# Second attention of a two-block kernel: the values' projection, the norm and the next logits taken into the pairs

## Reference, cut to what matters

```
proj = rms_norm(h, norm1_g) @ w_in_2
a_b, a_c, a_h, q, k, v, c_u, c_v = split(proj)
q = rms_norm(q per head, q_norm_g) ; k = rms_norm(k per head, k_norm_g)
for each block of 128 queries:
    z = (q @ k.T) / 8                     # keys up to the block's end
    log_beta = log_sigmoid(z)
    log_rem  = where(s < t, log_sigmoid(-z), 0)
    suffix   = reversed cumulative sum of log_rem, exclusive
    weights  = where(s < t, exp(log_beta + suffix), 0)
    o = weights @ v
```

## Time and profile before

| what | value |
|---|---|
| runs | 2827.7, 2827.54, 2825.6 us; median 2827.54 |
| profiled execution | 2826.8 us, its span 2824.7 us |
| mean granted clock of PE | 0.993 |
| PE busy | 2744.4 us, 97% of the span |
| DVE, ACT, POOL busy | 1892.2 (67%), 1006.8 (36%), 1187.7 us (42%) |
| chain that ended last | PE 82%, DVE 8%, issue 3%, POOL 3%, ACT 3%, DMA 1% |
| second attention | about 1588.7 to 1865.3 us of the span |

### The profile page before, as it was taken

One profiled execution on the slowest core, in us unless ns is written; L12 is line 12 of the kernel. 1 busy time (PEld: TensorE's weight loads), 2 busy tenths in 40 slices (PEclk: granted clock), 3 DMA queues, 4 the chain that ended last, 5 costly groups with the idle time before them and its releaser, 6 DMA issues.

```text
span 2824.7 us, 37570 instructions
## 1 busy us (share of the span) xinstructions
PE 2744.4 (97%) x14914; PEld 2208.4 (78%) x14914; DVE 1892.2 (67%) x2244; ACT 1006.8 (36%) x1482; POOL 1187.7 (42%) x705
## 2 busy tenths in 40 slices
PE   8999999989899999999999999999999999999999
PEld 6888777767778888888878666678778888888887
DVE  7677577677866777766768777655865545555555
ACT  5455433332422222222253455432332332232251
POOL 3111100002466766667764311132555555555553
PEclk9999999999999999999999999999999999999999
DMA  3111011121111111111112100012111111111112
GB/s 123 33 42 35 31 46 45 38 85 40 41 49 53 57 60 49 53 49 56 60 57 97 46 23 24 23 43 99 45 50 55 49 56 49 52 53 49 60 60 74
DMA packets 62760, 148.99 MB, mean 53 GB/s; under 512 B 7881, under 2 KB 8705, under 8 KB 62593
## 3 DMA queue, kind: packets, MB, share of 16 engines
q1 hardware_dynamic: 58272, 132.58, 14.9%
q10 hardware_dynamic: 4320, 14.09, 1.3%
HBM read 135.77 MB, written 8.52 MB: 51 GB/s over the span
## 4 chain that ended last, share of the span: by engine, by line
PE 82%; DVE 8%; issue 3%; POOL 3%; ACT 3%; DMA 1%; SPq 0%; ACTq 0%; DVEq 0%; POOLq 0%
PE ps L987 8%; PE ps L989 8%; PE ps L988 8%; PE ps L1109 8%; PE ps L1111 8%; PE ps L1110 8%; PE ps L1150 6%; PE ps L1152 6%; PE ps L1151 6%; PE ps L1274 2%; POOL ss L879 1%; PE ps L1490 1%; PE ps L1500 1%; PE ps L1514 1%; PE ps L1368 1%
## 5 line engine op out<-in xcount | busy, mean ns | idle before, releaser
L987 PE MATMUL ps<-a_hi,w_hi 128*128 128x512 f32 x1184 | 492.2, 416 | 10.6 <-POOL w_lo L856 10.0
L851 POOL TENSOR_TENSOR w_hi<-w_raw,der 128x1024 fp32r<-128x1024 f32 (+1 forms) x57 | 105.9, 1858 | 885.3 <-PE ps L989 766.3
L989 PE MATMUL ps<-a_hi,w_lo 128*128 128x512 f32 x1184 | 465.9, 393 | 0.0
L988 PE MATMUL ps<-a_lo,w_hi 128*128 128x512 f32 x1184 | 465.1, 393 | 0.0
L898 POOL TENSOR_TENSOR w_lo<-w_raw,w_hi 128x512 fp32r<-128x512 f32 x214 | 324.5, 1519 | 268.4 <-ACT w_hi L2457 268.4
L2132 DVE TENSOR_TENSOR x<-ps,x 128x512 f32<-128x512 f32 x432 | 295.4, 689 | 149.4 <-PE ps L1152 146.2
L2457 ACT ACTIVATE w_hi<-w_raw 128x512 fp32r<-128x512 f32 (+1 forms) x251 | 170.3, 680 | 540.1 <-PE ps L1152 238.0
L987 PEld LDWEIGHTS ps<-a_hi,w_hi 128*128 128x128 f32 x1184 | 224.6, 190 | 60.3 <-issue 17.5
L989 PEld LDWEIGHTS ps<-a_hi,w_lo 128*128 128x128 f32 x1184 | 223.9, 189 | 49.2
L988 PEld LDWEIGHTS ps<-a_lo,w_hi 128*128 128x128 f32 x1184 | 225.0, 190 | 37.3 <-issue 0.2
L898 POOL TENSOR_TENSOR w_lo<-asum,w_hi 128x512 fp32r<-128x512 f32 x114 | 166.6, 1461 | 185.0 <-ACT w_hi L2457 185.0
(11 more groups left out here) (395 smaller groups left out, 6113.5 us busy)
## 6 DMA issues: line engine op xcount, KB each, us to landing
w_raw<-in_w_mix SPq DMA_DIRECT2D x54, 512.0 KB, 3.7
w_raw<-in_w_f SPq DMA_DIRECT2D x96, 256.0 KB, 2.6
w_raw<-in_w_gu SPq DMA_DIRECT2D x88, 256.0 KB, 2.6
w_raw<-in_w_ple SPq DMA_DIRECT2D x16, 512.0 KB, 3.6
chunk<-in_w_f SPq DMA_DIRECT2D x32, 256.0 KB, 3.0
chunk<-in_w_dn SPq DMA_DIRECT2D x22, 256.0 KB, 3.0
w_raw<-in_w_dn SPq DMA_DIRECT2D x22, 256.0 KB, 3.0
x<-in_x SPq DMA_DIRECT2D x8, 512.0 KB, 7.5
```

Source lines behind the costliest of these rows:

```text
L987: mm(ps[:, bank, :], wh, hi[:, k, cols], start=(k == 0), stop=False)
L988: mm(ps[:, bank, :], wh, lo[:, k, cols], start=False, stop=False)
L989: last = mm(ps[:, bank, :], wl, hi[:, k, cols], start=False, stop=(k == nk - 1))
```

## The change

- `sb_fill` gives three units instead of two to the slots of pairs 0 to 2, so the next pair's values' unit is filling too (48 steps); `sb_slots` gives 3 steps to each of slots 0 to 7, 2 to slots 8 to 11, 1 to slots 12 to 15, 2 to slots 16 and 17 and 1 to slots 18 to 25.
- The block between pairs is gone from PE's list. What it did for pair 0 stands once ahead of the loop.
- ACT squares q in round 4 and k in round 6 and takes the root at the end of round 8. PE sums the squares in slot 14 (round 7) into bank 1. DVE takes the mean in round 7, the reciprocal in round 9 and the two multiplications at the end of round 11.
- For pairs 1 to 3 the factors are no longer spread by matmuls: SP writes them to DRAM after the reciprocal and reads them back with four transfers of 256 KB each (1 MB in all, 64 partitions by 4 pieces of 1 KB) into a new tile `spread_qk` of 8 KB a partition, which DVE's multiplications read in place of PSUM.
- The next pair's first two logits are made in round 12 as soon as q and k are ready, ahead of the last slot; in round 0 the first slot's filling comes ahead of the transposes of the values for pairs 1 to 3.
- SP's loop over the weights of this stage is written out, and waits for the factors ahead of the load of a values' unit.

```diff
 def sb_fill(p):
-    return (U_SB + 3 * (p + 1), 2) if p + 1 < HEADS else (U_CV, 3)
+    return (U_SB + 3 * (p + 1), 3)
 ...
-    return [[steps.pop(0) for _ in range(2 if i < 2 or 15 <= i < 19 else 1)] for i in range(n)]
+    counts = [3] * 8 + [2] * 4 + [1] * 4 + [2] * 2 + [1] * 8
+    return [[steps.pop(0) for _ in range(m)] for m in counts]
+S_SUM = 14
 ...  SP
-            weights("w_mix2", U_SB, U_OUT2 - U_SB)
+            def spread_qk_factors(p):
+                sp_.wait_ge(st_inv, N_QK + p + 1)
+                sp_.dma_start(qk_factors[p - 1].rearrange("r g c -> (r g) c"), hsm[0:P:8, :]).then_inc(qk_fac_out, 16)
+                sp_.wait_ge(qk_fac_out, 16 * p)
+                sp_.wait_ge(qk2_ready, 2 * p)
+                for t in range(2):
+                    for hh in range(2):
+                        src = qk_factors[p - 1, :, 2 * t + hh, :].rearrange("(o r) c -> o r c", o=1)
+                        sp_.dma_start(spread_qk[64 * hh:64 * hh + 64, t, :].rearrange("p (r c) -> p r c", r=4),
+                                      src.to_broadcast([64, 4, T // 4])).then_inc(qk_fac_in, 16)
+            for u in range(U_SB, U_OUT2):
+                p, t = divmod(u - U_SB, 3)
+                if t == 2 and 2 <= p <= HEADS:
+                    spread_qk_factors(p - 1)
+                sp_.wait_ge(w_split, u - 1)
+                sp_.dma_start(w_raw[:, u % 2, :], io["w_mix2"][u - U_SB]).then_inc(w_in[u % 2], 16)
 ...  PE, in round n of pair p
+                    if n == 0:
+                        if p:
+                            norm_fill(p, slots[0])
+                        pe.wait_ge(acc_free, half_no(u + 2, 1))
+                        pe.wait_ge(swt_ready, 2 * NSEG * p)
+                        pe.wait_ge(so_out, 2 * p)
+                        transposes(sv, 6, sv_tr)
+                        if p == 0:
+                            norm_fill(p, slots[0])
+                        norm_fill(p, slots[1])
+                        continue
                     for hh in range(2):
-                        if 1 <= n <= NSEG:
+                        if n <= NSEG:
                             turn(p, n - 1, hh)
-                        if n <= NSEG:
+                        if n == NSEG and hh and more:
+                            pe.wait_ge(qk2_ready, 2 * p + 4)
+                            logits(p + 1, 0)
+                            logits(p + 1, 1)
+                        if n <= NSEG and more:
+                            norm_fill(p, slots[2 * n + hh])
+                            if 2 * n + hh == S_SUM:
+                                pe.wait_ge(sq_qk, 2 * p + 4)
+                                pe.wait_ge(acc_free, half_no(u + 4, 1))
+                                head_sums(1)
+                        elif n <= NSEG:
                             fill(slots[2 * n + hh])
 ...  DVE, after the weights of round n
+                    if p + 1 < HEADS:
+                        if 2 * n == S_SUM:
+                            head_mean(N_QK + p + 1, 1)
+                        elif 2 * n == S_SUM + 4:
+                            head_factor(N_QK + p + 1)
                     evict(slots[2 * n] + slots[2 * n + 1], u_next, next_)
+                    if p + 1 < HEADS and 2 * n == S_SUM + 8:
+                        dve.wait_ge(qk_fac_in, 64 * (p + 1))
+                        for t, gain in enumerate((dcol("qn"), col("kn"))):
+                            stt(sk[(p + 1) % 2][:, t, :], sk[(p + 1) % 2][:, t, :], gain, spread_qk[:, t, :],
+                                ALU.mult, ALU.mult).then_inc(qk2_ready, 1)
 ...  ACT, end of round n
-                    if n == 10 and p + 1 < HEADS:
-                        square(p + 1, 0)
-                if p + 1 < HEADS:
-                    square(p + 1, 1)
+                    if p + 1 < HEADS:
+                        if n in (4, 6):
+                            square(p + 1, n // 2 - 2)
+                        elif n == 8:
+                            head_sqrt(N_QK + p + 1)
```

More of the change, by code:

```diff
@@ L95 @@
 SPREAD = tuple(range(N_DA, N_HG + HEADS - 1))
+SPREAD_QK = tuple(range(N_QK + 1, N_QK + HEADS))
 def bc_no(n):
-    return n + 1 - len([m for m in SPREAD if m <= n])
+    return n + 1 - len([m for m in SPREAD + SPREAD_QK if m <= n])
 F_MIX = 0
@@ L416, in bass_two_blocks @@
         hsm = at("hsm", T // 4, S0 + 57 * KB)
+        spread_qk = at("spread_qk", (2, T), -15 * KB)
         past = at("past", T, TMP)
@@ L486, in bass_two_blocks @@
         x_back = nc.dram_tensor("x_back", (P, KT, T), F32, kind="Internal").ap()
+        qk_factors = nc.dram_tensor("qk_factors", (HEADS - 1, 4, 4, T // 4), F32, kind="Internal").ap()
         factors = nc.dram_tensor("factors", (len(SPREAD), KT, P), F32, kind="Internal").ap()
@@ L512, in bass_two_blocks @@
         fac_in = sem("fac_in")
+        qk_fac_out = sem("qk_fac_out")
+        qk_fac_in = sem("qk_fac_in")
         guarded = sem("guarded")
@@ L1039, in gemm_loop, with head_sums @@
                         gemm(u0 + 2 * i + s, s, hi, lo, nk, wait_k if s == 0 else None)
-            def head_sums():
+            def head_sums(bank=7):
                 for g, src in enumerate((c_buf, ss)):
                     for r in range(4):
-                        last = mm(ps[32 * r:32 * r + 32, 7, 0:256], heads[g], src[:, 256 * r:256 * r + 256],
+                        last = mm(ps[32 * r:32 * r + 32, bank, 0:256], heads[g], src[:, 256 * r:256 * r + 256],
                                   start=g == 0, stop=g == 1, skip_group_check=True)
@@ L1517, in values, with norm_fill @@
                 last.then_inc(so_mm, 2)
+            def norm_fill(p, slot):
+                for step in slot:
+                    if step == (U_SB + 3 * (p + 1) + 2, 1, 0):
+                        pe.wait_ge(st_var, N_QK + p + 2)
+                    fill([step])
+            gemm_half(U_SB + 2, 1, U_SB % 2, a_hi, a_lo, KT, end=3)
+            pe.wait_ge(sq_qk, 2)
+            head_sums()
+            gemm_half(U_SB + 2, 1, U_SB % 2, a_hi, a_lo, KT, first=3, end=6)
+            pe.wait_ge(xf_ready, 1)
+            head_bcast(N_QK)
+            gemm_half(U_SB + 2, 1, U_SB % 2, a_hi, a_lo, KT, first=6)
+            pe.wait_ge(qk2_ready, 2)
+            logits(0, 0)
+            logits(0, 1)
             for p in range(HEADS):
                 u = U_SB + 3 * p
[L1521 to L1536, removed]
+                more = p + 1 < HEADS
                 slots = sb_slots(p)
[L1538 to L1541, removed]
                 for n in range(NSEG + 2):
@@ L1662, in prep, with head_mean, head_factor, head_inverse @@
                 tt(ss[:, :], ss[:, :], sq[:, k % 2, 0:T], ALU.add).then_inc(ss_ready, 1)
-            def head_inverse(n):
+            def head_mean(n, bank=7):
                 dve.wait_ge(st_sum, n + 1)
-                ts(hsm[:, :], ps[:, 7, 0:256], 1.0 / 64, EPS, ALU.mult, ALU.add).then_inc(st_var, 1)
+                ts(hsm[:, :], ps[:, bank, 0:256], 1.0 / 64, EPS, ALU.mult, ALU.add).then_inc(st_var, 1)
+            def head_factor(n):
                 dve.wait_ge(st_root, n + 1)
                 nc.vector.reciprocal(hsm[:, :], hsm[:, :]).then_inc(st_inv, 1)
+            def head_inverse(n):
+                head_mean(n)
+                head_factor(n)
             def row_inverse(n, scale):
@@ L2343, in _ @@
             dve.wait_ge(tri_in, 32)
-            for p in range(HEADS):
[L2345 to L2353, removed]
+            leave_half(U_SB + 2, 0, sv[:, :], 4)
+            head_inverse(N_QK)
+            dve.wait_ge(st_bc, bc_no(N_QK))
+            for t, gain in enumerate((dcol("qn"), col("kn"))):
+                stt(sk[0][:, t, :], sk[0][:, t, :], gain, banks(4 - 2 * t), ALU.mult, ALU.mult).then_inc(qk2_ready, 1)
+            leave_half(U_SB + 2, 1, sv[:, :])
+            dve.wait_ge(x_out, 16 * KT)
+            for p in range(HEADS):
                 slots = sb_slots(p)
@@ L2356, in _ @@
                 if p + 1 < HEADS:
-                    next_ = [sk[(p + 1) % 2][:, 0, :], sk[(p + 1) % 2][:, 1, :]]
+                    next_ = [sk[(p + 1) % 2][:, 0, :], sk[(p + 1) % 2][:, 1, :], sv[:, :]]
                 else:
                     next_ = [cc[:, j, :] for j in range(3)]
-                dve.wait_ge(x_out, 16 * KT)
                 for n in range(NSEG + 1):
@@ L2366, in _ @@
                         weights(p, n, 1)
-                    evict(slots[2 * n] + slots[2 * n + 1], u_next, next_)
+                    if p + 1 < HEADS:
[3 more added lines that the diff above has]
+                            head_factor(N_QK + p + 1)
+                    evict(slots[2 * n] + slots[2 * n + 1], u_next, next_)
+                    if p + 1 < HEADS and 2 * n == S_SUM + 8:
+                        dve.wait_ge(qk_fac_in, 64 * (p + 1))
+                        for t, gain in enumerate((dcol("qn"), col("kn"))):
+                            stt(sk[(p + 1) % 2][:, t, :], sk[(p + 1) % 2][:, t, :], gain, spread_qk[:, t, :],
```

(5 more changed lines are left out.)

## The result

The changed kernel takes 2836.63 us (median of 6 runs, 2834.72 to 2839.78) against 2825.85 us before in the same comparison: 1.0037 times as long, 95% interval 1.0027 to 1.0047. That is 10.8 us slower, where no measurable change (2823.8) was forecast, and above the range of 2816.5 to 2832.

A forecast was written before the change was run, and what follows sets the result against it. PE, busy 97% of the span, was taken as the bound: periods of 69.55 us against 70.70 give -3.45 over three, the last pair -0.3, so -3.75 and a median of 2823.8 us, range 2816.5 to 2832.

The forecast's parts named there:

- the transfer: Factors through DRAM to DVE's multiplications in round 11: 8.3 us from reciprocal to use, 7.95 available, so 0.35 us late.
- the upper bound of 11.9: Highest estimate of the factors' way through DRAM, if a 1 KB packet takes as long as an average 2.3 KB one.
- The first block's 5.38 us: Precedent in the profile before: from reciprocal to what waits for it, 512 KB in rows of 4 KB.
- the sum: A period of 65.0 + 0.35 + 3.85 + 0.35 = 69.55 us against 70.70; with the last pair -3.75 us in all.
- The price of a late transfer: At pair ends: slower by over 5.7 us only from about 3 us late; below that nothing measurable changes.
- the far end: Factors 3.95 us late: period 73.15 us, plus 1.6 us of slow clock each time, +11.9 us in all, 2839.
- Rival 2: The four factor transfers come late at DVE's round 11 multiplications, up to 2839 us; chance 0.10 from 3 us on.
- The tail: Rounds 8 to 13 of a pair: DVE has no rest and PE waits for it; 3.85 us a period.
- The last pair: Final pair of the stage: loses its 0.85 us table load, has thinner first slots; -0.3 us kept.
- Rival 1: DVE doesn't bound rounds 8 to 13: period 66.1 us, 2813.4 in all, half way 2818.5; chance 0.37 with half way.
- Rival 3: Each ACT table switch costs about 1.4 us more than its load: +4.6 us in all, 2832; chance 0.02.
- rival 4: Waits in mid-pair (values' unit half 1, squares in round 6) hold PE up; ends at no change; chance 0.03.

## Why the prediction was wrong

**The step that failed is the transfer**, "so I take 8.3". From the end of the reciprocal to DVE's use it measured 11.0, 9.8 and 11.3 us, so the upper bound of 11.9 was the nearer one. The pieces, for pair 1: 1.8 for the write, 1.95 until the last of four reads is issued (about 0.65 each), 6.0 from there to landing; in pair 0 3.5, 2.0 and 5.4. The first block's 5.38 us had one read and one short write in it, and I had put only a little more than the bytes on top of it. Bytes and issues together are shown by the run with half the reads, pieces of 1 KB (0.1 to 1.1 us) by that with 4 KB rows, and the load behind them (0.3 to 0.9 us), of which the sum says nothing, by the one with its order turned. So DVE was late by 2.2 to 3.7 us, not 0.35.

**The price of a late transfer was too low as well.** I counted the clock's 1.6 us a time at the far end, 3.95 us late, but the sentence that nothing measurable changes below about 3 us leaves it out: at 2.9 us late the terms of the sum give 3 x 1.4 - 0.3 = +3.9 us, and with the clock, which I had seen fall after 3.48 us of standing still, +8.7. It fell after 3.25, 2.10 and 1.91 us too (after the last, with half the reads, a pair's first to third logits took 9.53 us instead of 8.01). Without that, the direct lateness alone (PE's waits sum to 12.4 us against 2.8 without the transfer, 9.6 more) would have used up the gain of 4.9 and left 4.7; with 5.8 of clock it is 10.5, against 10.8 measured. Rival 2 is what happened. I had put 2839 at its far end and gave it a chance of 0.10 from 3 us on. It deserved far more: the estimate stood on one precedent of half the size, and its upper bound lay beyond that point.

**The tail was right for DVE.** Zero at the start of round 9 (1710.94 in the profile after): the scans of segment 9 were put at 2.85 and came at 2.98, the end of the reciprocal at 8.35 and 8.3, the last weights at 16.3 and 15.9. At the turn of segment 10 PE waited 0.56 us instead of 1.4: it came there 0.6 later than I had it, not least by a wait of 0.64 at the turn of segment 8, where ACT's copy stands behind the table loads and which the walk of PE leaves out. Without lateness the sum gives a period of 69.20 and -4.8 us; without the transfer 68.94 and -4.9 were measured. That the two agree so closely is partly luck: two errors nearly cancel. PE's waits are 2.1 us a pair (0.64, 0.57 and 0.93) instead of my 3.2 (1.4, 0.3 and 1.5), and what PE needs beside them is 66.8 instead of 66.0. The table loads had their share in it (5.8 us) and the reciprocal too (5.5), each taken away alone. That the block's removal would pay for itself only just, since DVE becomes the bound at the pair's end, is shown.

**The last pair** went as put: without the transfer, its 66.22 us from first logits to the end hold 0.69 and 1.02 moved in from the pair before, which leaves 64.5 against 64.80, -0.3. In the changed kernel the slow clock at its start makes it 68.01.

**Rival 1** (the tail isn't bound by DVE) was wrong for the change as made and right for what could be made of it: with the reciprocal moved into DVE's idle time, periods of 67.4 and 66.95 us against its 66.1. **Rival 3** (a drain at each table switch) and **rival 4** (waits in mid-pair) are excluded by the timelines: no gap after a load, no wait of PE in rounds 0 to 8 of pairs 1 and 2.

## What to carry to other kernels

A result that goes through DRAM has a due time: add the write up to its landing, each issue and the last read's landing separately, at the size and number they have, and put its producer where its engine idles anyway, several us before the need. When PE bounds the kernel and has to stand still even for some 2 us, count the slow stretch behind it too; here it cost 5.8 us on top of 9.6 of waiting. And where a list is moved into the shadow of another, walk the engine that gets the new work to the end of the stage: it may become the bound in the last rounds although on average it has a quarter of its time free (54.3 of 73.7 us busy here).

## What the runs showed of the hardware

- In this stage the granted clock fell after PE had stood still for 1.91, 2.10 and 2.52 us and in all seven cases of 3.25 to 4.74 us (means of 0.50 to 0.75 over the next 5 to 6 us), and that cost 1.4 to 2.8 us each time, from first to third logits; after 0.93 and 1.06 us it stayed at 1.00.
- The same write of 16 KB landed in about 1.8 us or in 3.05 to 3.5 us: at all three boundaries in 1.8 with the early reciprocal (both kernels that have it and a transfer), in the other profiles longer behind pair 0, 1.8 behind pair 1, and either behind pair 2. The cause is open, and nothing was tried for it; in the changed kernel the core moved no other data (0 GB/s) in the last microsecond before each of the three.
- Each of the four reads occupied SP's queue for about 0.65 us (2.6 for the four), and a load behind them still slowed their landing by 0.3 to 0.9 us.
- A switch of ACT's table cost ACT its 1.28 us and a gap of at most 0.02 us.
